# The second block's scans with each level's eight chunks as two rows of four

## The reference, cut to what matters

```python
h = rms_norm_2(x, norm_pre[layer])
proj = h @ w_in[layer]
y_a = gla_branch(...)    # 4 heads of 32: a gated scan forwards and one backwards
y_b = diff_branch(...)   # 4 heads: softmax(q0 k0) - lam * softmax(q1 k1), times v
y_c = hgrn_branch(...)   # 4 heads of 64: a gated scan forwards and one backwards
x = x + rms_norm_2(concatenate([y_a, y_b, y_c]) @ w_out[layer], norm_post[layer])

def chunked_gated_scan(q, k, v, log_g):
    """S_t = diag(exp(log_g_t)) S_{t-1} + k_t^T v_t ; o_t = q_t S_t"""
```

## Time and profile before

| | |
|---|---|
| median of 3 runs | 4637.75 us (4632.31 to 4640.51) |
| profiled execution, its own time | 4640.63 us |
| its span | 4638.7 us |
| granted TensorE clock over the span | 0.915 |
| PE, DVE, ACT, POOL busy | 84%, 44%, 31%, 22% |

### The profile page before, as it was taken

One profiled execution on the slowest core, in us unless ns is written; L12 is line 12 of the kernel. 1 busy time (PEld: TensorE's weight loads), 2 busy tenths in 40 slices (PEclk: granted clock), 3 DMA queues, 4 the chain that ended last, 5 costly groups with the idle time before them and its releaser, 6 DMA issues.

```text
span 4638.7 us, 66428 instructions
## 1 busy us (share of the span) xinstructions
PE 3902.2 (84%) x29046; PEld 2418.3 (52%) x29346; DVE 2036.1 (44%) x2160; ACT 1438.2 (31%) x1794; POOL 1007.3 (22%) x442
## 2 busy tenths in 40 slices
PE   5988899999989999777995977979685877978776
PEld 2555565665656654345443555555452455555443
DVE  3456455455444551412224254263734254264642
ACT  4222323323233221311113323434443232343442
POOL 2313333233332321111131101111023200111013
PEclk9999999999999999888997988989897978989888
DMA  2111111111111113223222100100011100100011
GB/s 89 51 38 38 52 38 47 47 51 52 38 51 38 51 65 141 77 95 114 104 69 74 33 10 9 42 14 28 19 59 61 33 10 10 41 19 19 23 50 55
DMA packets 61585, 226.93 MB, mean 49 GB/s; under 512 B 6832, under 2 KB 8560, under 8 KB 60784
## 3 DMA queue, kind: packets, MB, share of 16 engines
q1 hardware_dynamic: 50064, 181.77, 11.3%
q10 hardware_dynamic: 11232, 40.90, 2.2%
HBM read 174.93 MB, written 47.71 MB: 48 GB/s over the span
## 4 chain that ended last, share of the span: by engine, by line
PE 68%; DVE 17%; ACT 10%; issue 2%; POOL 2%; DMA 1%; ACTq 0%; DVEq 0%; SPq 0%; POOLq 0%
PE psum L886 66%; DVE arena L1925 6%; ACT arena L1419 6%; DVE arena L1928 5%; DVE arena L2355 2%; DVE arena L2292 2%; POOL arena L2401 2%; PE psum L889 1%; ACT L1419 1%; DVE arena L1932 1%; ACT hh L1419 1%; ACT wh L1419 1%; ACT arena L1866 1%; DVE hl L1925 1%; POOL wl L2401 0%
## 5 line engine op out<-in xcount | busy, mean ns | idle before, releaser
L886 PE MATMUL psum<-arena 64*64 64x32 f32 (+12 forms) x19058 | 1595.4, 284 | 505.9 <-DVE arena L1925 199.8
L886 PEld LDWEIGHTS psum<-arena 64*64 64x64 f32 (+6 forms) x19058 | 1114.5, 160 | 994.4 <-issue 512.3
L2401 POOL TENSOR_TENSOR wl<-arena,wh 128x1024 bf16<-128x1024 f32 (+1 forms) x195 | 474.7, 2435 | 2436.2 <-ACT wh L1419 2434.2
L886 PE MATMUL psum<-hh,wh 128*128 128x512 f32 x3120 | 890.3, 432 | 121.8 <-ACT hh L1419 72.9
L1419 ACT ACTIVATE arena<-psum 128x512 f32<-128x512 f32 (+4 forms) x660 | 415.8, 630 | 1242.5 <-PE psum L886 960.2
L886 PEld LDWEIGHTS psum<-hh,wh 128*128 128x128 f32 x3120 | 609.0, 201 | 330.6 <-ACT hh L1419 85.1
L1925 DVE TENSOR_TENSOR arena<-psum,arena 128x512 f32<-128x512 f32 (+3 forms) x488 | 319.4, 654 | 980.0 <-PE psum L886 635.1
L886 PE MATMUL psum<-hh,wl 128*128 128x512 bf16 (+1 forms) x2911 | 727.9, 392 | 20.7 <-issue 7.4
L886 PE MATMUL psum<-hl,wh 128*128 128x512 bf16 (+1 forms) x3029 | 717.6, 383 | 10.6 <-issue 8.1
L1928 DVE SCALAR_TENSOR_TENSOR arena<-arena 128x1024 f32<-128x1024 f32 (+1 forms) x388 | 610.1, 1572 | 118.4 <-ACT arena L1419 103.4
L1925 DVE TENSOR_TENSOR arena<-arena 128x1024 f32<-128x1024 f32 (+9 forms) x514 | 434.3, 845 | 371.2 <-ACT arena L1419 209.2
(11 more groups left out here) (30 smaller groups left out, 819.5 us busy)
## 6 DMA issues: line engine op xcount, KB each, us to landing
arena<-in_w_in SPq DMA_DIRECT2D x161, 512.0 KB, 3.5
scr_g<-arena ACTq DMA_DIRECT2D x24, 512.0 KB, 2.6
arena<-scr_g SPq DMA_DIRECT2D x24, 512.0 KB, 4.6
arena<-in_w_out SPq DMA_DIRECT2D x24, 512.0 KB, 3.5
arena<-in_w_mem_kv SPq DMA_DIRECT2D x16, 512.0 KB, 3.5
scr_x<-arena SPq DMA_DIRECT2D x16, 512.0 KB, 2.6
arena<-scr_x SPq DMA_DIRECT2D x16, 512.0 KB, 7.3
arena<-in_x SPq DMA_DIRECT2D x8, 512.0 KB, 10.3
```

The lines of the kernel that those rows point to most:

```text
L886: return pe.e.matmul(o, l, r, start=start, stop=stop)
L2401: return pool.seq.tensor_tensor(o, a, b, op)
```

## The change

Every level is cut into two rows, g = 0 (chunks 0 to 3) and g = 1 (chunks 4 to 7), each with its own `xk`, `lev` and `grow` and its own semaphore values. `xk` becomes twice two copies of 128x256 per level, `grow` twice six instructions over half as many elements. Row g of level lv+1 no longer waits for row 1-g of level lv. `grow(lv, g)` now stands ahead of the `leve` of the last part of its own row; for HGRN, with one part a row, that is every part. The two yields of a level that held no part of it go (GLA 6 to 4 per level, HGRN 4 to 3), one yield is put into `attend` between `qk` and `dmax`, and PACE and BESIDE are lower to match.

```diff
+            for g in range(2):
+                do("xk", L, t, 0, g)
+            yield
             for lv in range(7):
-                do("xk", L, t, lv)
-                yield
                 for g, p in parts:
                     held(("lev", L, t, lv, g, p), ("lev", L, t, lv, g, p))
                     yield
-                    if (g, p) == parts[-1]:
-                        do("grow", L, t, lv)
+                    if p == nh // 2 - 1:
+                        do("grow", L, t, lv, g)
+                    elif g and lv < 6:
+                        do("xk", L, t, lv + 1, 0)
+                    elif not g and lv:
+                        do("xk", L, t, lv, 1)
                     do("leve", L, t, lv, g, p)
                     ps.leave(("lev", L, t, lv, g, p))
-                yield
+                if not gla and lv < 6:
+                    do("xk", L, t, lv + 1, 0)
+                    yield
+                    do("xk", L, t, lv + 1, 1)
...
             do("qk", L, h, q)
+            yield
             for c in range(2):
                 do("dmax", L, h, q, c)
             yield
...
-    PACE = (0.6, 0.57, 0.54, 0.54)
+    PACE = (0.45, 0.45, 0.43, 0.44)
...
-                other.step(BESIDE[h][q] / 6)
+                other.step(BESIDE[h][q] / 7)
...
-            if (g, p) == (0, 0):
-                pe.wait_ge(*at("xk", L, t, lv))
...
+            pe.wait_ge(*at("xk", L, t, lv, g))
+            if lv == 0:
+                pe.wait_ge(*at("qf_dve", L, t))
+                pe.wait_ge(*at("qf_pool", L, t))
+            else:
+                pe.wait_ge(*at("grow", L, t, lv - 1, g))
...
-        def xk(L, t, lv):
+        def xk(L, t, lv, g):
...
             if lv == 0:
-                act.wait_ge(*at("diag", L, t, 1, 1 if t == 0 else 0))
-                act.wait_ge(*at("qf_dve", L, t))
-                act.wait_ge(*at("qf_pool", L, t))
+                act.wait_ge(*at("diag", L, t, g, last))
+                act.wait_ge(*at("KG", L, t, 1))
...
-        def grow(L, t, lv):
+        def grow(L, t, lv, g):
...
-            dve.wait_ge(*at("xk", L, t, lv))
-            dve.wait_ge(*at("lev", L, t, lv, 1, 1 if t == 0 else 0))
-            m = 1 << lv
+            dve.wait_ge(*at("lev", L, t, lv, g, heads(t) // 2 - 1))
+            m, n, cc = 1 << lv, 256 >> lv, slice(512 * g, 512 * g + 512)
             for d in range(2):
+                T, k, q = tree(d, lv)[:, n * g:n * g + n, :], half(KG[d][:, cc], d, m), half(QF[d][:, cc], 1 - d, m)
+                tt(k, k, T[:, :, 1 - d:2 - d].to_broadcast([128, n, m]), MUL).then_inc(*dve.up("grow_k", L, t, lv, g, d))
+                tt(q, q, T[:, :, d:d + 1].to_broadcast([128, n, m]), MUL).then_inc(*dve.up("grow_q", L, t, lv, g, d))
...
```

More of the change, by code:

```diff
@@ L787, in attend @@
             yield
-    PACE = (0.6, 0.57, 0.54, 0.54)
-    BESIDE = ((1, 2, 3, 2, 3, 3, 3, 2), (5, 6, 4, 3, 0, 0, 1, 6), (3, 4, 3, 4, 3, 1, 0, 0), (0, 2, 3, 3, 3, 2, 2, 0))
+    PACE = (0.45, 0.45, 0.43, 0.44)
+    BESIDE = ((1, 2, 2, 3, 3, 3, 3, 2), (5, 5, 2, 1, 1, 2, 4, 5), (3, 4, 3, 2, 2, 1, 2, 3), (2, 3, 3, 3, 2, 1, 1, 1))
     def mix(L):
@@ L1233, in lev @@
             cleared(use)
-            if (g, p) == (0, 0):
-                pe.wait_ge(*at("xk", L, t, lv))
-                if lv == 0:
-                    pe.wait_ge(*at("qf_dve", L, t))
-                    pe.wait_ge(*at("qf_pool", L, t))
-                else:
-                    pe.wait_ge(*at("grow", L, t, lv - 1))
+            pe.wait_ge(*at("xk", L, t, lv, g))
[4 more added lines that the diff above has]
+                pe.wait_ge(*at("grow", L, t, lv - 1, g))
             for c in range(4 * g, 4 * g + 4):
@@ L1252, in kt @@
             cleared(use)
-            pe.wait_ge(*at("grow", L, t, 6))
+            pe.wait_ge(*at("grow", L, t, 6, g))
             for c in range(4 * g, 4 * g + 4):
@@ L1783, in hz_gate @@
             ps.give(p, ("hz_g", L, t, d))
-        def xk(L, t, lv):
-            k, m = (ks, qq)[lv % 2], 1 << lv
+        def xk(L, t, lv, g):
+            k, m, cc, last = (ks, qq)[lv % 2], 1 << lv, slice(512 * g, 512 * g + 512), 1 if t == 0 else 0
             if lv == 0:
-                act.wait_ge(*at("diag", L, t, 1, 1 if t == 0 else 0))
-                act.wait_ge(*at("qf_dve", L, t))
-                act.wait_ge(*at("qf_pool", L, t))
-            else:
-                if lv > 1:
-                    act.wait_ge(*at("lev", L, t, lv - 2, 1, 1 if t == 0 else 0))
-                act.wait_ge(*at("grow", L, t, lv - 1))
-            f(half(k, 0, m), half(KG[0], 0, m), AF.Copy).then_inc(*act.up("xk0", L, t, lv))
-            f(half(k, 1, m), half(KG[1], 1, m), AF.Copy).then_inc(*act.up("xk", L, t, lv))
+                act.wait_ge(*at("diag", L, t, g, last))
+                act.wait_ge(*at("KG", L, t, 1))
+            else:
+                act.wait_ge(*at("grow", L, t, lv - 1, g))
+                if lv == 1:
+                    act.wait_ge(*at("qf_dve", L, t))
+                    act.wait_ge(*at("qf_pool", L, t))
+                    act.wait_ge(*at("diag", L, t, g, last))
+                else:
+                    act.wait_ge(*at("lev", L, t, lv - 2, g, last))
+            f(half(k[:, cc], 0, m), half(KG[0][:, cc], 0, m), AF.Copy).then_inc(*act.up("xk0", L, t, lv, g))
+            f(half(k[:, cc], 1, m), half(KG[1][:, cc], 1, m), AF.Copy).then_inc(*act.up("xk", L, t, lv, g))
         def kt(L, t, d, g):
@@ L1800, in kt @@
             act.wait_ge(*at(*use))
-            act.wait_ge(*at("lev", L, t, 6, 1, 1 if t == 0 else 0))
+            act.wait_ge(*at("lev", L, t, 6, g, 1 if t == 0 else 0))
             f(cols3((qq, ks)[d], 8)[:, 4 * g:4 * g + 4, :], cols3(bank(use), 4), AF.Copy).then_inc(*act.up("kt_copy", L, t, d, g))
@@ L2293, in leve @@
             ps.give(use, ("ATl", *use))
-        def grow(L, t, lv):
+        def grow(L, t, lv, g):
             if lv == 0:
                 dve.wait_ge(*at("qf_pool", L, t))
-            dve.wait_ge(*at("xk", L, t, lv))
-            dve.wait_ge(*at("lev", L, t, lv, 1, 1 if t == 0 else 0))
-            m = 1 << lv
+            dve.wait_ge(*at("lev", L, t, lv, g, heads(t) // 2 - 1))
+            m, n, cc = 1 << lv, 256 >> lv, slice(512 * g, 512 * g + 512)
             for d in range(2):
-                T = tree(d, lv)
-                tt(half(KG[d], d, m), half(KG[d], d, m), T[:, :, 1 - d:2 - d].to_broadcast([128, 512 >> lv, m]), MUL).then_inc(*dve.up("grow_k", L, t, lv, d))
-                tt(half(QF[d], 1 - d, m), half(QF[d], 1 - d, m), T[:, :, d:d + 1].to_broadcast([128, 512 >> lv, m]), MUL).then_inc(*dve.up("grow_q", L, t, lv, d))
-                x = tt(tree(d, lv + 1, True).unsqueeze(2), T[:, :, 0:1], T[:, :, 1:2], MUL)
-                x.then_inc(*dve.up(*(("grow", L, t, lv) if d else ("grow_0", L, t, lv))))
+                T, k, q = tree(d, lv)[:, n * g:n * g + n, :], half(KG[d][:, cc], d, m), half(QF[d][:, cc], 1 - d, m)
+                tt(k, k, T[:, :, 1 - d:2 - d].to_broadcast([128, n, m]), MUL).then_inc(*dve.up("grow_k", L, t, lv, g, d))
+                tt(q, q, T[:, :, d:d + 1].to_broadcast([128, n, m]), MUL).then_inc(*dve.up("grow_q", L, t, lv, g, d))
+                x = tt(tree(d, lv + 1, True)[:, n * g:n * g + n].unsqueeze(2), T[:, :, 0:1], T[:, :, 1:2], MUL)
+                x.then_inc(*dve.up(*(("grow", L, t, lv, g) if d else ("grow_0", L, t, lv, g))))
         def st(L, t, d):
```

## The result

The changed kernel takes 4708.38 us (median of 4 runs, 4706.95 to 4709.29) against 4635.95 us: the ratio is 1.0155 with a 95% interval of 1.0138 to 1.0173. It is slower by 72 us. The forecast was 4646 us in a range of 4560 to 4705: the time lies outside of the range, though on the side that had the larger chance by a hair.

The account below looks back on a forecast made before the run. The prediction took PE, busy for 84% of the span, as the bound, with its idle time and slow clock to win. Terms summed to +4 us a layer, +8 on 4640.6; less 2.9 for the median, 4646 us, range 4560 to 4705.

Parts of the forecast that it names:

- (a): Levels: the chain grow, xk, lev cut in rows shortens PE's waits for ACT: -34 us a layer.
- (b): Behind the last level: kt waits only for row 1's grow and leve: -4 us a layer.
- (c): Levels: two half instructions cost DVE more than one whole: +12 us a layer.
- (e): Softmax: the yield puts scan steps ahead of dmax on DVE, so dt waits longer for dexp: +9 us a layer.
- (f): Last turns: the scan ends about a turn earlier, so nothing fills the softmax chain there: +5 us a layer.
- (d): Levels: leve behind grow gives its pair back 2.3 us later at 21 places: +16 us a layer.
- The slower rival: Turns with levels: DVE becomes the bound there, 4690 us in all, chance 0.25.
- The clock: Level stretches: each us of PE idle time that goes or comes moves another 0.46 us; cancels in the forecast.

Follow-up runs that it names:

- rows_old_plan: Kernel before with xk and grow cut in rows, each row's grow behind its own leve, old yields and tables: 4613.77 us, ratio 0.9944.
- rows_yield: rows_old_plan with a yield added between qk and dmax, PACE times 6/7, BESIDE over 7: 4582.72 us, ratio 0.9876.
- leve_first: The changed kernel with each row's last leve ahead of its grow, nothing else: 4641.10 us, ratio 1.0016.
- both: The changed kernel without the yield between qk and dmax, with leve ahead of grow, PACE and BESIDE's divisor scaled: 4699.48 us, ratio 1.0135.
- halves: Kernel before with xk and grow each as two halves at their old places, old yields and tables: 4638.16 us, ratio 1.0008.
- row0_leve_first: The changed kernel with leve ahead of grow in row 0 alone: 4676.02 us, ratio 1.0079.
- before_leve_first: Kernel before, grow whole, with leve ahead of grow at a level's last part: 4694.61 us, ratio 1.0118.

## Why the prediction was wrong

The runs give a path from the kernel before to the changed one, with one part added at a time. The prediction's terms sort onto it, doubled for two layers:

| part | predicted us | measured us | from |
|---|---|---|---|
| rows, `leve` first: (a) + (b) + (c) | -52 | -26 | `rows_old_plan` |
| the yield: (e) | +18 | -32 | `rows_yield` over it |
| loop with fewer yields, PACE, BESIDE: (f) | +10 | +65 | `leve_first` over it |
| `grow` ahead of `leve`: (d) | +32 | +64 | the changed kernel over it |
| sum | +8 | +72 | |

The sum is 64 us too low. The rows gain half of what they were given (26 us missing), and giving a pair back behind `grow` costs 32 us more than charged, because the term (d) left row 1 out: 58 us. Two larger misses, 55 us for the loop and 50 us the other way for the yield, leave 5, which is luck. That split depends on the order in which the parts are added: with the loop first, from `rows_old_plan` to `both`, it costs 89 us, and the yield in it (`both` to `leve_first`) then gains 55.

*(a) The mechanism was right, its worth too high.* The level matmuls wait 14.0 us for ACT where about 10 were forecast and 42.6 stood. (a), (b) and (c) together are worth 26 us in place of 52, in the old plan. `halves` has the same fall of ACT's waits and no gain: 16.2 of 30.5 us came back as waits for `leve` and 10.1 as waits for other DVE work. The prediction priced the wait that goes and not fully what is late next.

*(b) did not hold.* `kt` still waits for a `leve`, 8.8 us in three places against 5.9 in one; at 3129.27 it is 5.1 us.

*(c) Sizes about right, the price open.* DVE grew by 54 us (40 forecast), ACT by 17 (16). `halves`, with the split instructions alone, has 41 us more on DVE, so the forecast's size is right for them; the other 13 go with work of GpSimd (last section). What the 41 us cost by themselves no run shows; with row 0's earlier `xk` they come to 4 us, against the 24 charged. The slower rival, DVE as the bound of the level turns, did not hold as a cause. Its signs came half true (DVE at 74% and 80% of the HGRN windows, and a PE that waits mostly for DVE), and its time, 4690 us, came nearer than the forecast's. But `leve_first` has the same DVE work in the same turns and is 64 us faster, with DVE still busier in the HGRN levels, and what the loop costs lies where DVE is idle for most of the time (69.59 us busy in 216 between the levels of t = 0 and t = 1). In the levels PE waits for the place of one DVE instruction in the queue, not for the sum of DVE's work.

*(d) is a step that failed: it counted row 0 alone.* A pair that comes free 2.3 us later at 21 places was charged at a third, 16 us a layer, 32 in all. Those very places cost 35 us (`row0_leve_first`), so the price that was set on them was right. But the waits for `leve` grew by 25.4 us rather than 15, and exchanging the two lines in both rows gave back 64 us: the other 29 come from row 1, whose order the prediction took for unchanged and free. Before the change that order was the better one by 55 us (`before_leve_first`), since the whole chain hung on it. Cut in rows, the chain no longer needs it, and the pair that is given back late costs as it does in row 0.

*(e) failed by its sign: right about the wait, wrong about the edit.* `dt` waits 26.9 us for `dexp` (15 or more forecast), and `both` against `leve_first` shows that in the new loop the yield makes 28.5 us of what is 12.8 without it; in the old loop it adds nothing (8.7 against 8.0 and, with rows, 14.2 against 13.9). In the queue of ACT, too, steps stand ahead of `dexp` that the prediction had not looked for. Ahead of the longest wait:

```profile
2976.99 1.06 ACT L1428 ACTIVATE wh<-arena 128x1024 fp32r<-128x1024 f32 x1 [15.64 <-PE psum L896]
2978.07 1.28 ACT L1428 ACT_TABLE_LOAD   x1
...
2979.36 2.08 ACT L1428 ACTIVATE arena<-psum 128x1024 f32<-128x1024 f32 x2
...
2982.81 1.11 ACT L1879 ACTIVATE arena<-psum,arena 128x1024 f32<-128x1024 f32 x1
...
2984.07 1.97 PE L899 MATMUL psum<-arena 128*128 128x128 f32 x8 [7.16 <-ACT arena L1879]
```

A weight's copy waits 15.64 us for PE at the head of ACT's queue, and `dexp` stands behind it. Still the yield gains 30 to 61 us in all four kernels, and in all four the idle time in the levels falls, by 12 to 20 us a layer; that this is because a seventh place spreads the scan's steps is argued and not shown. The prediction listed what the yield delays and never what it does for the scan: an addition of a place is a change of pace too.

*(f) and the loop: the largest miss of the table.* The sign that was named did not show: behind the last `qk` PE idles 2.12 + 1.70 + 0.94 + 1.45 + 2.35 = 8.6 us up to the first closing projection, before 8.2, where over 12 were forecast. The turns ahead of the last one lose instead. From the last level matmul on, the kernel before idles 14.1 us in 76 and the changed one 22.1 in 104, so the 5 us of (f) were no bad size for this. But the fewer yields a level and the lower PACE had no term beside (f) and a part of (c), and the loop, PACE and BESIDE together cost 65 us. The windows show where the idle time lies: inside of the level windows it is 32.9 + 33.6 + 35.9 = 102.4 us, as much as before (40.4 + 27.8 + 36.6 = 104.8), and outside of them 177.2 - 102.4 = 74.8 us, against 155.2 - 104.8 = 50.4. The levels go through fewer turns (turn 0 of head 2 now takes 32 us from `qk` to `qk`, and 24 before), and the stretches between and behind them wait longer: from 2815 to 3031 `dt` waits 9.0 us for `dexp` and the matmuls 14.8 us for DVE's multiplications, where it was 1.5 and 3.9.

*The clock.* The level windows have 0.82, 0.81 and 0.82, within the 0.80 to 0.88 forecast. 22 us of idle time brought 10.4 us of busy time, 0.47 us for each, and 0.46 was assumed: this price fits, and it did not cancel since the idle time did not. It is a mean and not a constant: from `leve_first` to the changed kernel 30.8 us more idle time in layer 0's mixing brought no busy time (663.1 and 663.2), from the kernel before to `before_leve_first` 12.6 us brought 11.6.

What stays open: how the 65 us divide between the missing yields and the lower PACE, which were not run apart; by what the yield gains; and why the order in row 1 matters in the one loop and not in the other. The sum of the table is exact by construction; along another path its parts would be other numbers (the rows are worth +50 us with `grow` first).

## What to carry to other kernels

When a chain is cut into rows that run side by side, try the instruction that gives the shared bank back ahead of the chain's next step; when nothing runs beside the chain, behind it: here the same two lines were worth 64 and 76 us one way, 55 us the other. Ask it of every row, also of the one whose order the edit leaves alone. A wait that goes is worth only what remains after the next thing in that engine's queue is ready; ask which buffer that needs. Where an edit adds or drops places of a weave, price what the new spacing does to both generators, not only what it delays: here the two such edits moved the time by -32 and +65 us, and the forecast had +18 and +10.

## What the runs showed of the hardware

DVE instructions with two inputs from SBUF took longer beside work of GpSimd. In the turn above, the six multiplications of a row take 4.20 us beside a GpSimd instruction that runs from 3078.52 to 3081.18; those of the row at 3072.70 take 2.33. The same on one instruction of the kernel before, which follows one of the same size with an input in PSUM:

```profile
3262.96 1.22 DVE L1925 TENSOR_TENSOR arena<-psum,arena 128x1024 f32<-128x1024 f32 x1
3264.22 2.19 DVE L1925 TENSOR_TENSOR arena<-arena 128x1024 f32<-128x1024 f32 x1
```

```profile
3262.99 2.34 POOL L2401 TENSOR_TENSOR arena<-arena 128x1024 f32<-128x1024 f32 x1 [25.70 <-DVE arena L1932]
```

The first runs beside the GpSimd instruction from its start and keeps its 1.22 us; the second has both inputs in SBUF, takes 2.19 and ends 1.08 us behind the end of the GpSimd instruction (3265.33). Counted over the whole trace of the changed kernel, 121 of the 512 DVE instructions that overlap GpSimd work take over a quarter longer than the median of the same instruction (174 us in all), and none of the 1900 others, nor any of the 236 that overlap it with an input in PSUM. In the kernel before it is 161 us in all, so 13 of the 54 us that DVE has more are these. In layer 0's mixing it is 10.1 us before and 14.6 after, in layer 1's 7.9 and 16.7, while both grow by 33 us: a small part of the result at most, and most of what made 6.78 us of the 4.6. The Trainium skill ("SBUF — State Buffer", "SBUF: two separate sides") has this as a rule: DVE work with two SBUF inputs and GpSimd work that reads SBUF exclude each other for a whole instruction. The two places shown and the instructions with an input in PSUM agree with it. The prediction should have looked at what GpSimd does beside each `grow`.
